# Latent attention layer: one filling order for every head, and the rotary staging begun one tile sooner

## The reference, cut to what matters

```
q = (rmsnorm(c_q, q_norm_g) @ w_uq)     # per head: 128 plain + 64 rotary columns
kv = (rmsnorm(c_kv, kv_norm_g) @ w_ukv) # per head: 128 key + 128 value columns
for i in range(S // BLOCK_Q):           # 8 query tiles of 128 tokens
    s = q_nope[i] @ k_nope[:k_end].T + q_rope[i] @ k_rope[:k_end].T
    p = softmax(where(causal, s * scale, -inf))
    o[i] = p @ v[:k_end]
return (o * silu(g)) @ w_out
```

## Time and profile before

| | |
|---|---|
| median of three runs | 2669.32 us |
| the profiled execution | 2669.93 us, of which the span of its instructions is 2668.2 us |
| PE busy | 2400.2 us (90% of the span) |
| DVE busy | 1530.2 us (57%) |
| ACT busy | 1322.1 us (50%) |
| granted TensorE clock, mean | 0.961 of full speed |
| the first and the last score matmul of the latent layer | 605.1 and 1373.3 us from the start |

### The profile page before, as it was taken

How to read it: one execution, slowest core, us unless ns; L and a number is a source line. 1 busy time by engine, 2 the same in 40 slices (tenths; PEclk the granted TensorE clock), 3 DMA queues, 4 the chain that set the end, 5 groups by cost and what they waited for, 6 DMA issues and landing times. The chain is left out here.

```text
span 2668.2 us, 42519 instructions
## 1 busy us (share of the span) xinstructions
PE 2400.2 (90%) x17068; PEld 1361.1 (51%) x17068; DVE 1530.2 (57%) x2164; ACT 1322.1 (50%) x1989; POOL 361.3 (14%) x266
## 2 busy tenths in 40 slices
PE   8999988977879988988988999999998899999887
PEld 4667744434444544544544455555554346776543
DVE  5555464665556565565647566566666365546555
ACT  4433333444544454454544678777777444233332
POOL 0000001120100001001002233233323210000001
PEclk9999999999989999999999999999999899999999
DMA  3001102213433342342431211111210111101113
GB/s 113 33 33 41 33 32 79 81 35 63 86 69 73 83 86 69 83 90 67 96 78 58 72 44 45 48 56 48 56 48 31 57 65 41 40 33 36 37 49 119
DMA packets 199768, 160.29 MB, mean 60 GB/s; under 512 B 160114, under 2 KB 165490, under 8 KB 199572
## 3 DMA queue, kind: packets, MB, share of 16 engines
q1 hardware_dynamic: 199572, 157.56, 22.3%
HBM read 98.79 MB, written 4.19 MB: 39 GB/s over the span
## 5 line engine op out<-in xcount | busy, mean ns | idle before, releaser
L240 PE MATMUL psum<-h_hi,w_hi 128*128 128x512 f16 x1128 | 433.3, 384 | 11.3 <-DVE mla_kn_lo L619 8.6
L241 PE MATMUL psum<-h_lo,w_hi 128*128 128x512 f16 x1128 | 432.5, 383 | 0.0
L242 PE MATMUL psum<-h_hi,w_lo 128*128 128x512 f16 x1128 | 431.9, 383 | 0.0
L2260 DVE SCALAR_TENSOR_TENSOR w_lo<-wf,w_hi 128x1024 f16<-128x1024 f32 (+3 forms) x194 | 232.5, 1205 | 155.5 <-ACT w_hi L2255 155.2
L256 PE MATMUL psum<-w_hi,h_hi 128*128 128x128 f16 x1504 | 256.9, 219 | 0.0
L257 PE MATMUL psum<-w_lo,h_hi 128*128 128x128 f16 x1504 | 256.6, 219 | 0.0
L258 PE MATMUL psum<-w_hi,h_lo 128*128 128x128 f16 x1504 | 256.6, 219 | 0.0
L1612 ACT ACTIVATE ssum<-psum,mla_neg_top 128x128 f32<-128x128 f32 (+7 forms) x128 | 94.5, 738 | 266.8 <-DVE mla_neg_top L1521 266.5
L1097 POOL TENSOR_TENSOR sb_al<-sb_zc,sb_ah 128x256 f16<-128x256 f32 (+2 forms) x96 | 166.2, 1731 | 372.3 <-ACT sb_ah L1062 372.3
L2255 ACT ACTIVATE w_hi<-wf 128x1024 f16<-128x1024 f32 (+3 forms) x194 | 187.5, 974 | 37.7 <-PE psum L242 19.3
L1533 DVE SCALAR_TENSOR_TENSOR mla_prob_halves<-ssum,mla_inv_total,mla_prob_halves 128x128 f16<-128x128 f32 (+7 forms) x128 | 116.4, 910 | 121.6 <-ACT mla_prob_halves L1620 121.6
(11 more groups left out here) (295 smaller groups left out, 5623.2 us busy)
## 6 DMA issues: line engine op xcount, KB each, us to landing
wf<-in_gla_out SPq DMA_DIRECT2D x32, 512.0 KB, 3.5
wf<-in_sb_in SPq DMA_DIRECT2D x32, 512.0 KB, 3.4
wf<-in_mla_out SPq DMA_DIRECT2D x20, 512.0 KB, 3.9
wf<-in_gla_v SPq DMA_DIRECT2D x16, 512.0 KB, 3.5
wf<-in_gla_g SPq DMA_DIRECT2D x16, 512.0 KB, 3.5
wf<-in_mla_gate SPq DMA_DIRECT2D x16, 512.0 KB, 3.9
wf<-in_sb_out SPq DMA_DIRECT2D x16, 512.0 KB, 3.5
xT<-in_x_T SPq DMA_DIRECT2D x16, 256.0 KB, 5.7
```

Of the source, the lines that this page charges most:

```text
L240: pe.matmul(out, wh[:, w], act_hi[:, k, tok], start=(i == 0), stop=False)
L241: pe.matmul(out, wh[:, w], act_lo[:, k, tok], start=False, stop=False)
L242: mm = pe.matmul(out, wl[:, w], act_hi[:, k, tok], start=False, stop=(i == last))
L2260: dve.scalar_tensor_tensor(out=self.w_lo[s % Layer.NSPLIT][:, 0:cols], in0=self.wf[s % Layer.NLOAD][:, 0:cols], scalar=W_SCALE, in1=self.w ...
```

## The change

The two strings, one for the first head of each group of four and one for the rest, become a single one. Letters of units that a head does not have are skipped.

```
-    ORDER = "uxuxuxuuxugrgr", "uuuguuugxrxxrx"
+    ORDER = "uuguuguuxxrxxr"
...
-        turns = [k for k in self.ORDER[h % self.GROUP == 0] if k in made]
+        turns = [k for k in self.ORDER if k in made]
...
-            if h % 2 and h + 1 < MLA_HEADS and 2 <= i < 6:
-                main += self.stage_items(h + 1, range(2 * i - 4, 2 * i - 2))
+            if h % 2 and h + 1 < MLA_HEADS and 1 <= i < 5:
+                main += self.stage_items(h + 1, range(2 * i - 2, 2 * i))
```

## The result

Over twenty executions of each kernel the changed one takes 2672.81 us in the median (2669.87 to 2677.75) and the kernel before 2669.07 us (2664.33 to 2672.72). The ratio is 1.0017, with a 95% interval of 1.0011 to 1.0023. That is slower by 0.17%, some 4 us: less than the 0.3% that the chances went by, inside the range of 2642 to 2685, but on the other side of the forecast, which was 4.5 us faster.

What follows compares the result with a forecast made beforehand. The prediction took the chain of DVE and ACT, nearly as long as PE's work, as the bound. Terms -6.4 - 3.1 + 6 + 1.5 - 1.5 = -3.5 us, taken as -4.5 from 2669.93, gave 2665 us; range 2642 to 2685.

Steps and rivals of the forecast that it cites:

- the chances: Whole kernel: 0.32 faster, 0.43 same, 0.25 slower; a change under 0.3%, 8 us, counts as the same.
- PE's gaps are not the time: Latent layer: PE's 30.3 us of staging waits are not 30.3 us of time; gain bounded by DVE's 39.5 us.
- The rival at 2640: Latent layer: PE's gaps were the cost, so removing its waits pays in full, 30 of 39.5 us; 2640 us, chance 0.17.
- A gate in line costs 3.5 us: Tiles 2 and 3: a gate ahead of a reciprocal or maximum costs DVE 3.5 us, against about 1 for most before.
- The sum: Latent layer: changes added by heads give -3.5 us, taken as -4.5, from the profiled 2669.93 us.
- The rest of heads 4 to 15: Four pairs from head 6 on -6.4 us, heads 4 and 5 -3.1, head 14 +1.5, head 15 -1.5.
- all such new waits at 0.6 us a pair: Pairs of heads: new waits for PE, for banks, `yt` products and rotary multiplications, add 0.6 us, giving 101.5.
- Heads 1 to 3 ... +6: Heads 1 to 3, without output units: odd heads +4 each for gates, head 2 -2.5, slab splits +0.5; +6 us.
- one more microsecond of gain: Whole layer: -4.5 us taken instead of -3.5, since sums by instruction came out a little under those by difference.
- Gates in line slow PE too: Heads 1 to 14: PE waits 1.4 us or more for a gate's copy, 1.5 us a head more; 2686 us, chance 0.18.
- Staging late: Turns of heads: staging DMAs still come late and PE's waits stay; 2672 us, chance 0.10.
- The bound on the loss: Latent layer: at most 49 us lost, 14 x 3.5, if gates cost 3.5 us twice a head against 1.

Runs made afterwards that it cites:

- `stage_only`: The changed kernel with the two old order strings back, so only the earlier staging is new against the kernel before; 2659.21 us, ratio 0.9968.
- `order_only`: The changed kernel with the staging put back where it was, so only the single new order string is new against the kernel before; 2700.71 us, ratio 1.0131.
- `short_gate_after`: The changed kernel with each gate's exponential, logarithm and exponential replaced by one copy (gate not computed); 2636.18 us, ratio 0.9875 to the kernel before.
- `short_gate_before`: The kernel before with each gate's exponential, logarithm and exponential replaced by one copy (gate not computed); 2649.20 us, ratio 0.9922.
- `gate_behind`: The changed kernel with each gate's clamp, activations and multiplication moved later, its copy left in place; 2644.96 us, ratio 0.9911 to the kernel before.
- `even_new`: The changed kernel with the new order only in even heads from 4 on, old order elsewhere, early staging; 2637.16 us, ratio 0.9887 to the kernel before.

## Why the prediction was wrong, point by point

- **PE's gaps are not the time.** Right beside the old order, not beside the new one. 30.3 us of staging waits became 0.9, and the layer grew; `stage_only` prices the loss of 27.5 of them at 8.5 us, a third. But `order_only` prices them at 30 us where they stand beside the new order, so the statement holds for the kernel before and not for the layer as such. The Trainium skill (Perfetto Trace Analysis, Identifying the Most-Contended Engine) names the engine with the highest occupancy. It adds, which the prediction leaves out, that for TensorE busy time is no good measure and that its headroom is to be judged by FLOPs and by the share of its weight loads. That share is 51% in the profile before, below DVE's 57%, so the skill's page doesn't plainly point at PE here. The rival at 2640 stands for working on PE's gaps, and it didn't come.
- **A gate in line costs 3.5 us.** Right in place and size. Tiles 2 and 3 were put at 17.0 and 18.6 us and took 17.07 and 18.50. The waits for `kn` and `v` hi parts rose by 45 us, and `short_gate_after` gave back what 28 gates in line should. Not all of the 28 are new, though: the second string had gates in line in heads 4, 8 and 12 already, where tiles 2 and 3 didn't grow. The sum is safe from this, since it subtracted whole pairs of known length. The old order's price, put at 1 us for most gates, was too low by `short_gate_before`; it was no term of its own in the sum for heads 6 and 7, whose thirds were counted by instruction.
- **The rest of heads 4 to 15.** Tiles 0 and 1 were put at 8 and 8.1 us and took 7.92 and 9.35, tiles 4 to 7 at 26.7 and 22.5 and took 26.41 and 22.02. The one number clearly off is that of the odd head's first two tiles (10.3 to 10.4 in heads 9, 11 and 13). There the `yt` multiplication waits for products of PE, which comes out of a 3.58 us wait for the rotary multiplications and then runs at half its clock (the last section has the rows). The prediction had put all such new waits at 0.6 us a pair. DVE's waits for `yt` are 22.0 us in 14, from 13.2 in 6, and the four pairs gained 4.2 us, not 6.4. Heads 4 and 5 gained 0.9 and not 3.1, head 14 lost 1.1 (put at 1.5), head 15, to its last row maximum, gained 0.8 (put at 1.5). Together these are 4.7 us short of the sum.
- **The step that failed: "Heads 1 to 3 ... +6".** It measured +12.0 in the trace, and 12 to 14 us by the experiments. Heads 1, 2 and 3 were put at +4, -2.5 and +4.5 and came to +4.5, +1.0 and +6.5. I had counted the two gates in line and not the tiles behind them. The windows of tiles 4 to 7 of head 2, first before and then after:

```profile
714.35:739.89 25.54, 19.34 (x142) 10.96 (x140) 15.67 (x24) 12.37 (x19) 4.36 (x3) 0.90 0.37 88
```

```profile
716.99:745.84 28.85, 20.70 (x160) 13.18 (x158) 19.00 (x31) 13.87 (x22) 2.42 (x2) 0.88 0.41 96
```

The stretch grew by 3.3 us and DVE's busy time in it by 3.3. On DVE's timeline of the two, two `v` lo parts (728.38 and 729.58 after) and a second set of rotary multiplications came in, which had stood in tiles 0 to 3, and two splits of 512 columns took the place of one of 1024. In heads 1 and 3, where tiles 4 to 7 grew by 1.5 and 2.3 us, PE waits 4.9 us each for a slab's split at their end (to 695.18 and 794.38), two waits that the kernel before did not have. Taken over the three heads, tiles 2 and 3 lost 10.7 us, tiles 4 to 7 lost 7.1, and tiles 0 and 1 gained 5.9. In the pair of heads 6 and 7 output additions left tiles 0 to 3 to make room, and cost little further back; heads 1 to 3 have no output units. The prediction named this and then priced the gates alone. That this is why the three heads pay more is read from the rows and was not tested by a run of its own. The short gates give a part of it: they take 10.0 us off heads 1 to 3 in the new order (147.6 to 137.6) and 2.8 in the old (135.7 to 132.9), so of the 12.0 us some 7 go with the length of the gates' activations and 4.7 stay without two of the three.
- **The sum.** -3.5 was forecast for the trace and +8.0 is the change of the layer's length; over the same heads as the forecast the trace has +7.2 (head 15's -0.8 lies behind the layer's last mark, +0.1 in head 0 before it). Of the 10.7 us between -3.5 and +7.2, 6.0 are heads 1 to 3 and 4.7 the rest, all on one side. The term taken without working, one more microsecond of gain because "the sums by instruction came out a little under those by difference", went the wrong way as well.
- **The rivals.** "PE's gaps" at 2640 fell with the result and `stage_only`, though `order_only` shows its price beside the new order. "Gates in line slow PE too" asked for 14 waits of 1.4 us or more for the gate's copy. There are 13, 20.0 us, 1.5 on average, and they stay in `gate_behind`, which is 28 us faster. Its price, 1.5 us a head beyond the sum, didn't come: heads 6 to 13 were put at 4 x 101.5 = 406.0 and took 408.2, 0.3 us a head more, and the rival needed 0.9. PE's clock in the pairs is 0.97 and 0.98, above the 0.94 to 0.97 of before. The prediction has from the Trainium skill (TensorE: Matmul & The Clock Gate, HAM oscillation) that by the page alone many small waits would leave the clock up. The same page of the Trainium skill also tells, in its next section, of a kernel whose short waits lowered the clock, so it is these rows, and not the page, that say so. "Staging late" is excluded by the 0.9 us.
- **Slips that moved nothing.** The longest of the seven waits was 6.0 us, not 5.5, and so longer than the 5.8 that the staging comes sooner; 0.9 us of waits are left, 0.3 of them at that turn. PE is busy 91 to 94 us of a pair, not 92 to 94. The bound on the loss should read 70 us and not 49: two gates a head at 3.5 us for 1 are 5 us a head, and there are 14 heads. It doesn't enter the sum.

What stays open: why the medians differ by 3.7 us where the two traces differ by 8.0 in the layer. In the profiles of the twelve kernels the layer's first maximum stands either at 601.7 to 603.2 us (eight of them) or at 606.0 to 606.4 (before, after, `order_only`, `even_new`), though none of the edits touches what runs ahead of it. Both shown traces are of the later kind. A median of many executions may mix the two; one profile of each kernel doesn't tell in which shares. It bears on the small numbers alone: by the layer's length the change costs 8.0 us, by medians 3.7.

## What to carry to other kernels

Before moving work on one engine to fill another's gaps, ask which chain the gap waits beside, and what an instruction that enters between two of its links has to wait for: here a chain of three activations that cost DVE 2.5 us at each of 28 places, on engines that were 57% and 49% busy. A rule that suits some heads should be tried by heads, and against the kernel that has the other half of the change: with the staging early in both, the new order won 19.2 us in heads 4, 8 and 12 together, 1.0 in heads 6 and 10, and cost 5.7 in head 7. And price a stretch that lacks what the order was made for (heads 1 to 3, without output units) by its own instructions, third by third, and not by analogy.

## What the hardware showed that I had not expected

- A transfer that comes sooner has no price of its own here. The same move of the staging DMAs gave 8.5 us beside one order and 30 beside the other. The rows of `order_only` put the difference down to what stands behind the late matmul.
- PE's half-rate stretches feed back on the chain. At the end of head 8 PE waits for the rotary multiplications, and behind the wait its clock is down. PE's timeline, a window of head 9 and DVE's timeline in the changed kernel:

```profile
1050.61 0.58 PE L240 MATMUL psum<-h_hi,w_hi 128*128 128x512 f16 x1 [3.58 <-DVE mla_rt L1495]
```

```profile
1052.86:1056.02 3.16, 3.16 (x13) 1.45 (x11) 2.15 (x5) 1.75 (x4) 0.00 (x0) 0.50 0.43 158
```

The granted clock is 0.50, 1.2 GHz, for those 3.16 us, and the matmuls from 1050.61 on, which took 0.58 to 0.63 us each where those before the wait took 0.38, were at that clock too. The product for `yt` came late by the wait and the slow stretch, and DVE waited for it:

```profile
1059.28 0.69 DVE L1543 TENSOR_TENSOR mla_yt<-psum,mla_silu_g 128x512 f32<-128x512 f32 x1 [2.49 <-PE psum L1439]
```

The wait for a gate's copy in tile 2 of head 6 left no such stretch: the clock of that third is 1.00 in the window 907.00 to 924.07 shown above. Its row:

```profile
909.07 0.38 PE L240 MATMUL psum<-h_hi,w_hi 128*128 128x512 f16 x1 [1.45 <-ACT mla_silu_g L285]
```

That agrees with what the Trainium skill says of idle stretches between bursts (TensorE: Matmul & The Clock Gate, HAM oscillation), as far as these lengths go.
